# Last group of an MLP's second layer in three passes of 352 tokens, with the norm and the store following pass by pass

## The reference, cut to what matters

```python
h2 = rms_norm(x, lp['norm_pre_mlp'])
ff = jnp.square(jax.nn.relu(h2 @ lp['mlp_w1'])) @ lp['mlp_w2']
x = x + rms_norm(ff, lp['norm_post_mlp'])
```

## Time and profile before

| | |
|---|---|
| Median of 3 runs | 2189.09 us (2188.5 to 2189.5) |
| The profiled execution | 2189.16 us |
| Its span, first to last instruction | 2187.4 us |
| Mean granted TensorE clock | 0.97 |
| Busy: PE, DVE, ACT, POOL | 2034.9, 953.0, 516.4, 708.4 us |

### The profile page before, as it was taken

One profiled execution on the slowest core, in us unless ns is written; L12 is line 12 of the kernel. 1 busy time (PEld: TensorE's weight loads), 2 busy tenths in 40 slices (PEclk: granted clock), 3 DMA queues, 4 the chain that ended last, 5 costly groups with the idle time before them and its releaser, 6 DMA issues.

```text
span 2187.4 us, 32684 instructions
## 1 busy us (share of the span) xinstructions
PE 2034.9 (93%) x13822; PEld 1915.7 (88%) x13822; DVE 953.0 (44%) x1204; ACT 516.4 (24%) x687; POOL 708.4 (32%) x352
## 2 busy tenths in 40 slices
PE   4999999999999978888999996799999999999993
PEld 4999899999898956567999995799999999999992
DVE  7894431244455425553355813842313222231336
ACT  4212211333343335554200112320101001010100
POOL 0231111111111123332456644443434433344340
PEclk8999999999999989999999997899999999999996
DMA  3323337366676423302344321211111111111123
GB/s 131 98 93 108 103 101 229 129 215 201 203 235 205 139 90 90 91 26 79 117 166 144 129 101 39 98 39 49 49 40 49 39 49 40 49 48 40 49 69 119
DMA packets 144563, 223.48 MB, mean 102 GB/s; under 512 B 33808, under 2 KB 98576, under 8 KB 144432
## 3 DMA queue, kind: packets, MB, share of 16 engines
q1 hardware_dynamic: 132336, 193.42, 28.3%
q10 hardware_dynamic: 12096, 28.12, 3.5%
HBM read 173.84 MB, written 45.56 MB: 100 GB/s over the span
## 4 chain that ended last, share of the span: by engine, by line
PE 88%; DVE 7%; issue 2%; ACT 1%; DMA 1%; POOL 0%; SPq 0%; DVEq 0%; POOLq 0%
PE ps L1484 75%; PE ps L1677 3%; PE ps L1713 2%; PE ps L1701 1%; DVE sm L1302 1%; PE ps L1504 1%; PE ps L1623 1%; DVE resid L1405 1%; PE ps L1585 1%; PE ps L1604 1%; DVE n_rstd L989 1%; ACT pt L856 1%; DVE n_tmp L1403 1%; PE ps L1513 1%; DVE n_sum L981 1%
## 5 line engine op out<-in xcount | busy, mean ns | idle before, releaser
L638 POOL TENSOR_TENSOR w_hi<-w_raw,zeros 128x1024 fp32r<-128x1024 f32 x94 | 227.1, 2416 | 588.3 <-PE ps L1484 532.9
L1484 PE MATMUL ps<-op_hi,w_hi 128*128 128x352 f32 x1536 | 345.8, 334 | 9.2 <-DVE op_lo L1345 4.9
L629 POOL TENSOR_TENSOR w_lo<-w_raw,w_hi 128x1024 fp32r<-128x1024 f32 x54 | 135.5, 2509 | 651.6 <-ACT w_hi L714 651.6
L1484 PE MATMUL ps<-op_lo,w_hi 128*128 128x352 f32 x1536 | 334.6, 326 | 0.0
L1484 PE MATMUL ps<-op_hi,w_lo 128*128 128x352 f32 x1536 | 333.0, 325 | 0.0
L1484 PEld LDWEIGHTS ps<-op_hi,w_hi 128*128 128x128 f32 x1536 | 261.0, 190 | 20.6 <-issue 14.4
L1484 PEld LDWEIGHTS ps<-op_lo,w_hi 128*128 128x128 f32 x1536 | 263.8, 189 | 0.0
L1484 PEld LDWEIGHTS ps<-op_hi,w_lo 128*128 128x128 f32 x1536 | 262.8, 189 | 0.0
L640 POOL TENSOR_TENSOR w_lo<-w_raw,w_hi 128x1024 fp32r<-128x1024 f32 x94 | 251.9, 2680 | 7.4
L1484 PE MATMUL ps<-hid_hi,w_hi 128*128 128x352 f32 x1056 | 230.1, 326 | 9.3 <-issue 8.6
L1484 PE MATMUL ps<-hid_lo,w_hi 128*128 128x352 f32 x1056 | 230.0, 326 | 0.0
(11 more groups left out here) (244 smaller groups left out, 2336.1 us busy)
## 6 DMA issues: line engine op xcount, KB each, us to landing
w_raw<-in_w SPq DMA_DIRECT2D x148, 512.0 KB, 3.6
kc<-in_k_cache SPq DMA_DIRECT2D x48, 448.0 KB, 5.2
vc<-in_v_cache SPq DMA_DIRECT2D x48, 448.0 KB, 6.6
out_keep<-stage ACTq DMA_DIRECT2D x24, 528.0 KB, 2.7
tmp_gate_d<-stage ACTq DMA_DIRECT2D x24, 528.0 KB, 4.0
gate_t<-tmp_gate_d SPq DMA_DIRECT2D x24, 528.0 KB, 3.7
qkv<-out_keep SPq DMA_DIRECT2D x18, 512.0 KB, 4.9
acc<-in_x SPq DMA_DIRECT2D x8, 528.0 KB, 6.6
```

What stands on the lines that cost most here:

```text
L629: pool.tensor_tensor(w_lo[:, b].rearrange("p k m -> p (k m)"), w_raw[:, b], w_hi[:, b].rearrange("p k m -> p (k m)").bitcast(F32), ALU.sub ...
L638: pool.tensor_tensor(hi.rearrange("p (a m) -> p a m", a=2), w_raw[:, b].rearrange("p (a m) -> p a m", a=2), zeros[:].unsqueeze(1).broadcas ...
L1484: mm = pe.matmul(ps[:, 3 * dst + q, 0:BLK], w[:, b, w0 + n], x[:, k, q * BLK:(q + 1) * BLK], start=(n == 0 and part == 0), stop=(n == len( ...
```

## The change

The last group (line 1801) no longer goes tile by tile over all tokens, but in three passes q of 352 tokens, each over the eight output tiles n. Since every pass needs all the weights, the four halves of the last two pairs are split into buffers of their own (`lw_hi`, `lw_lo`) in area B, as soon as the last `up` is done (`UP_DONE`) instead of when a half of `w_hi` has been read. The residual goes to `res_y`, also in area B, and its eight loads are issued behind the last weight load. The tiles use six single banks in turn (bank 6 is for the total of the squares), and a tile waits until DVE has added the one six before. DVE waits for both of GpSimd's last splits and all eight loads before its first sum. The sum of squares, total, root, reciprocal and the eight rows of a pass are written out between the tiles of the next pass (`LATER` says after which tile which row), and SP stores 24 pieces of 128 x 352 instead of 8 slabs.

```diff
+CH_USES = USES[P_MLP + 6] - USES[P_MLP + 2]
+UP_DONE = USES[P_MLP + 2] + (NCH - 2) * CH_USES + 2
+P_LAST = len(PAIRS) - 2
+LAST_BANKS = 6
+LATER = [[], [], [], [0], [1], [2], [3], [4]]
...
+        lw_hi = at("B", 0, "lw_hi", [P, 4, KD, P], F32R)
+        lw_lo = at("B", 16384, "lw_lo", [P, 4, KD, P], F32R)
+        res_y = at("B", 32768, "res_y", [P, KD, N])
+        ff_sq = [stage[:, 0, n * BLK:(n + 1) * BLK] for n in range(2)]
+        ff_rs = stage[:, 0, 2 * BLK:]
+        ff_tmp = w_raw[:, 0, 0:BLK]
...
 # SP
-            sy.wait_ge(mm_ready[0], USES[-1] - KD // 2 + 1)
+            for b in range(2):
+                sy.wait_ge(mm_ready[b], UP_DONE)
             for k in range(KD):
-                if k == FCH:
-                    sy.wait_ge(mm_ready[1], USES[-1])
-                    sy.wait_ge(mm_ready[0], USES[-1])
-                sy.dma_start(resid[:, k], t["x2_d"][:, k]).then_inc(x2_in, 16)
-            for k in range(KD):
-                sy.wait_ge(y_done, k + 1)
-                sy.dma_start(t["y"][:, k], resid[:, k]).then_inc(y_out, 16)
-            sy.wait_ge(y_out, 16 * KD)
+                sy.dma_start(res_y[:, k], t["x2_d"][:, k]).then_inc(x2_in, 16)
+            for q in range(NBLK):
+                for k in range(KD):
+                    sy.wait_ge(y_done, KD * q + k + 1)
+                    sy.dma_start(t["y"][:, k, piece(q)], res_y[:, k, piece(q)]).then_inc(y_out, 16)
+            sy.wait_ge(y_out, 16 * KD * NBLK)
...
 # GpSimd
-            with pool.Fori(0, NCH - 1) as c:
-                for n in range(4):
-                    pair(c * 4 + first + n, PAIRS[first + n - 1], c * per + USES[first + n - 1])
-            run(len(PAIRS) - 1, len(PAIRS))
+            with pool.Fori(0, NCH - 2) as c:
+                pairs_of(c, range(4))
+            pairs_of(NCH - 2, range(3))
+            pool.wait_ge(mm_ready[0], UP_DONE)
+            for m in range(4):
+                split(P_LAST + m // 2, m % 2, (1, UP_DONE), (lw_hi[:, m], lw_lo[:, m]))
...
 # ACT
-            squares(n_ff, acc, lambda k: act.wait_ge(mm_free[k % 2], USES[-1] - KD // 2 + k // 2 + 1))
-            root(n_ff)
+            for q in range(NBLK):
+                for n in range(KD):
+                    last_square(q, n)
+                    if q and n == 1:
+                        last_root(q - 1)
+            last_root(NBLK - 1)
...
 # DVE
-            sums(last + per, n_ff)
-            inverse_root(n_ff)
+            def last_sum(q, n):
+                x = KD * q + n
+                dve.wait_ge(last_mm, x + 1)
+                v.tensor_tensor(acc[:, n, piece(q)], acc[:, n, piece(q)], ps[:, x % LAST_BANKS, 0:BLK], ALU.add).then_inc(last_kept, 1)
...
+            def last_inverse(q):
+                dve.wait_ge(n_ff.rs, q + 1)
+                v.reciprocal(stage[:, 1, piece(q)], ff_rs).then_inc(n_ff.h, 1)
+                dve.wait_ge(n_ff.h, q + 1)
+                dve.wait_ge(last_kept, KD * (q + 1))
+
+            def last_row(q, k):
+                wait(dve, y_done, KD * q + k)
+                v.scalar_tensor_tensor(out=ff_tmp, in0=acc[:, k, piece(q)], scalar=gains[:, 3, k:k + 1],
+                                       in1=stage[:, 1, piece(q)], op0=ALU.mult, op1=ALU.mult).then_inc(last_rows, 1)
+                dve.wait_ge(last_rows, KD * q + k + 1)
+                v.tensor_tensor(res_y[:, k, piece(q)], res_y[:, k, piece(q)], ff_tmp, ALU.add).then_inc(y_done, 1)
+
+            for b in range(2):
+                dve.wait_ge(w_split[b], len(PAIRS))
             dve.wait_ge(x2_in, 16 * KD)
-            add_normed(n_ff, 3, y_done)
+            for q in range(NBLK):
+                for n in range(KD):
+                    last_sum(q, n)
+                    if q >= 2 and n == 0:
+                        last_row(q - 2, 5)
+                    if n:
+                        last_square(q, n - 1)
+                    if q >= 2 and n in (1, 2):
+                        last_row(q - 2, 5 + n)
+                    if q and n == 2:
+                        last_inverse(q - 1)
+                    if q:
+                        for k in LATER[n]:
+                            last_row(q - 1, k)
+                if q == NBLK - 1:
+                    last_row(q - 1, 5)
+                last_square(q, KD - 1)
+            for k in range(6, KD):
+                last_row(NBLK - 2, k)
+            last_inverse(NBLK - 1)
+            for k in range(KD):
+                last_row(NBLK - 1, k)
...
 # TensorE
-            down(p1 + 4 * c + 4, 1, FCH * (c + 2), u1 + (c + 1) * per)
-            sum_squares(n_ff, USES[-1])
+            def last_tile(q, n):
+                m, x = n // 2, KD * q + n
+                te.wait_ge(w_split[m % 2], P_LAST + m // 2 + 1)
+                if x < LAST_BANKS:
+                    te.wait_ge(mm_free[x // 3], u1 + (c + 1) * per)
+                else:
+                    te.wait_ge(last_kept, x - LAST_BANKS + 1)
+                for k in range(FCH):
+                    for part, (w, y) in enumerate(((lw_hi, mid_hi), (lw_hi, mid_lo), (lw_lo, mid_hi))):
+                        mm = pe.matmul(ps[:, x % LAST_BANKS, 0:BLK], w[:, m, FCH * (n % 2) + k], y[:, FCH + k, piece(q)],
+                                       start=(k == 0 and part == 0), stop=(k == FCH - 1 and part == 2))
+                mm.then_inc(last_mm, 1)
+
+            def last_total(q):
+                te.wait_ge(n_ff.added, KD * (q + 1))
+                wait(te, n_ff.rs, q)
+                pe.matmul(ps[:, 6, 0:BLK], ones[:], pre_rstd[:, piece(q)], start=True, stop=True).then_inc(n_ff.sum, 1)
+
+            te.wait_ge(hid_l, FCH * NCH)
+            for q in range(NBLK):
+                for n in range(KD):
+                    last_tile(q, n)
+                    if q and n == 1:
+                        last_total(q - 1)
+            last_total(NBLK - 1)
```

More of the change, by code:

```diff
@@ L208, in hybrid_layer, with piece @@
         mid_lo = at("A", AREA // 2, "mid_lo", [P, 2 * FCH, N], F32R)
+        lw_hi = at("B", 0, "lw_hi", [P, 4, KD, P], F32R)
[4 more added lines that the diff above has]
+        ff_tmp = w_raw[:, 0, 0:BLK]
+        def piece(q):
+            return slice(q * BLK, (q + 1) * BLK)
         class NormTiles:
@@ L353, in hybrid_layer @@
         go = sem("go")
+        last_mm, last_kept, last_rows = sem("last_mm"), sem("last_kept"), sem("last_rows")
         hid_z, hid_f, hid_h, hid_l, hid_r = (sem("hid_" + x) for x in ("z", "f", "h", "l", "r"))
@@ L630, in low_of, with split @@
                                    w_hi[:, b].rearrange("p k m -> p (k m)").bitcast(F32), ALU.subtract).then_inc(w_split[b], 1)
-            def split(i, b, used):
-                if used:
-                    pool.wait_ge(mm_ready[used[0]], used[1])
+            def split(i, b, used, to=None):
+                pool.wait_ge(mm_ready[used[0]], used[1])
                 pool.wait_ge(w_loaded[b], 16 * (i + 1))
-                hi, lo = (w[:, b].rearrange("p k m -> p (k m)") for w in (w_hi, w_lo))
+                hi, lo = (w.rearrange("p k m -> p (k m)") for w in (to or (w_hi[:, b], w_lo[:, b])))
                 pool.tensor_tensor(hi.rearrange("p (a m) -> p a m", a=2), w_raw[:, b].rearrange("p (a m) -> p a m", a=2), zeros[:].unsqueeze(1).broadcast_to([P, 2, KD * P // 2]), ALU.add).then_inc(w_half, 1)
@@ L683, in _, with pairs_of @@
             first, per = P_MLP + 3, USES[P_MLP + 6] - USES[P_MLP + 2]
-            with pool.Fori(0, NCH - 1) as c:
-                for n in range(4):
-                    pair(c * 4 + first + n, PAIRS[first + n - 1], c * per + USES[first + n - 1])
-            run(len(PAIRS) - 1, len(PAIRS))
+            def pairs_of(c, ns):
+                for n in ns:
+                    pair(c * 4 + (first + n), PAIRS[first + n - 1], c * per + USES[first + n - 1])
+            with pool.Fori(0, NCH - 2) as c:
[4 more added lines that the diff above has]
+                split(P_LAST + m // 2, m % 2, (1, UP_DONE), (lw_hi[:, m], lw_lo[:, m]))
         @block.scalar
@@ L959, in _, with last_square, last_root @@
                 hidden(FCH * (NCH - 1) + n, n, 1, stage[:, 0])
-            squares(n_ff, acc, lambda k: act.wait_ge(mm_free[k % 2], USES[-1] - KD // 2 + k // 2 + 1))
-            root(n_ff)
+            def last_square(q, n):
+                x = KD * q + n
+                act.wait_ge(last_kept, x + 1)
+                wait(act, n_ff.added, x - 1)
+                s.activation(ff_sq[x % 2], acc[:, n, piece(q)], ACT.Square).then_inc(n_ff.sq, 1)
+            def last_root(q):
+                act.wait_ge(n_ff.sum, q + 1)
+                wait(act, n_ff.h, q)
+                s.activation(ff_rs, ps[:, 6, 0:BLK], ACT.Sqrt, bias=EPS, scale=1.0 / D).then_inc(n_ff.rs, 1)
+            for q in range(NBLK):
[4 more added lines that the diff above has]
+            last_root(NBLK - 1)
         @block.vector
@@ L1466, in _, with last_square @@
             sums(last + 2)
-            sums(last + per, n_ff)
-            inverse_root(n_ff)
```

(15 more changed lines are left out.)

## The result

The changed kernel takes 2172.59 us (median of 4 runs, 2171.15 to 2173.63) against 2189.3 (4 runs, 2188.5 to 2192.88): a ratio of 0.992, 95% interval 0.9903 to 0.9937. Forecast was 2173.5, range 2167 to 2180. The profiled execution took 2173.45 us for a span of 2171.7.

What follows compares the result with a forecast made beforehand. TensorE bounds the kernel up to its last matmul, then DVE: gapless from 2122.8 for 46.3 us to 2169.1, plus 2.6 for the last store gives span 2171.7; with 1.76 outside and the median adjustment, 2173.5 us, range 2167 to 2180.

Steps and rivals of the forecast that it cites:

- TensorE to the start of DVE's gapless stretch: Last group from 2100.8 until TensorE ends pass 1's third tile at 2122.8, at 1.947 us per tile.
- DVE's 80 instructions: From 2122.8 DVE runs 14 sums, 15 adds, 3 reciprocals and 24 rows without a gap: 46.3 us, ending at 2169.1.
- The last store: Final store at the kernel's end is 176 KB, not 528: 2.6 us instead of 3.1, with landing about 2.2.
- one bank: Last group: 12 successive matmuls adding into a single bank cost nothing extra; upper bound 2 us.
- the slack of 7 us: Residual loads land at about 2105; TensorE needs DVE's first sum only at 2112.5, so the wait costs nothing.
- One cover: Last pass's total, root and waits lie beside two leftover rows of pass 1 (2.3 us) on DVE, so cost nothing.
- my upper bound of 1.30: Last pass's 352-column ones-matmul for the total of squares takes 0.62 us, or 1.30 at half clock.
- No overlap: Rival: short DVE instructions never start before their predecessor ends, 45 joints give nothing back; +3.6 us, 2177.1; chance 0.17.
- DVE keeps pace: Rival: short DVE instructions are cheaper, only the last pass follows TensorE's end at 2148.7; time 2167.7; chance 0.06.
- x2 late: Rival: residual loads land at 2116 to 2125, TensorE stalls at tile 6 for 4 to 13 us; 2177 to 2186; chance 0.05.
- splits late: Rival: GpSimd's weight splits don't come forward, TensorE stalls 18 us at tile 6; about 2191.8; chance 0.03.
- Fixed cost: Rival: each DVE instruction costs 0.42 us fixed or more, not 0.158, making the chain 21 us longer, 2194.5; chance 0.04.

Runs made afterwards that it cites:

- x_pass2: Changed kernel plus eight unused 352-column DVE adds, one ahead of each sum of the last pass; last 1056-column sum to span end 73.5 us, against 70.05.
- late_split: Changed kernel with GpSimd's last split held until the sixth tile of the last group; last 1056-column sum to span end 77.9 us, against 70.05.
- sq_pool: sq_pe with GpSimd doing two of the last pass's eight rows, ACT multiplying their gain in; 2174.17 us, ratio 0.9928.
- no_adds: Changed kernel without the 21 DVE adds of squares (norm wrong, only time used); last 1056-column sum to span end 66.4 us, against 70.05.
- rows_end: Changed kernel with all 24 rows behind the last pass instead of between tiles; last 1056-column sum to span end 81.4 us, against 70.05.
- tiles_only: Kernel before with only the four splits and eight residual loads brought forward, no passes; 2189.75 us against 2190.08, ratio 0.9999.
- x_pass0: Changed kernel plus eight unused 352-column DVE adds, one ahead of each sum of pass 0; last 1056-column sum to span end 70.04 us, against 70.05.
- sq_pe: Changed kernel with squares summed by TensorE matmuls instead of DVE adds, rows fitted into the next pass; 2172.35 us, ratio 0.9916.
- two_banks: Changed kernel with two output tiles made together per pass, their matmuls alternating between two banks; last 1056-column sum to span end 73.2 us, against 70.05.
- blocks: Changed kernel with the other products also going block by block of 352 tokens into one bank, not three in turn; 2172.14 us.

## Why the prediction was right

**The sum, term by term.** By S I had forecast 2171.7 - 2100.82 = 70.9; it is 70.05. TensorE to the start of DVE's gapless stretch: 22.0 forecast, 21.7 measured (a tile takes 1.92, not 1.947; the inline total cost 0.59). DVE's 80 instructions: 46.3 forecast, 46.1 measured; the add 0.52, the scalar form 0.58, the reciprocal 2.35 are what the line through other sizes and the row of the very size said; one of the 15 adds is a copy of 0.34, which I had priced as an add. The last store: 2.6 forecast, 2.3 measured, because 176 KB land in 1.8, not 2.2. That the two spans both read 2171.7 is partly luck: this execution reached the last group 0.8 us later than the one of before.

**Removed, added, moved.** The matmuls cost nothing extra in one bank. The splits ended at 2088, 2093, 2098 and 2103 for 2087, 2092, 2097 and 2102. The residual was there at about 2107.6, not 2105: the loads issued at 2094.0 and took 13.6 us where I had taken 12; the slack of 7 us was 4 to 5, and the cost was nothing, as said. TensorE ended at 2149.1 for 2148.7. One cover was thinner than I thought: the root ended at 2157.58 and DVE started the last reciprocal at 2157.64, so 0.06 us more would have shown. The ones-matmul took 1.54, over my upper bound of 1.30. That this term cost nothing is in part luck.

**The rivals.** *No overlap*: the sum at 2128.52 lasts 0.51 and the next instruction starts at 2128.95, 0.08 ahead of its end, just as at 1056 columns. The Trainium skill's section "The DRAIN you can't avoid" goes on to say that an instruction that is not held starts earlier; I had left that out of the rival, and these rows agree with it, not with the sentence that I took. *DVE keeps pace*: no, a gapless 46 us; x_pass2 shows it from the other side. *x2 late* and *splits late*: neither came about, but late_split shows that I had them too cheap, since I priced a stall without the clock: 5.0 forecast for it, 7.9 measured. *Fixed cost*: an add of 352 columns takes 0.52, so it has the 0.158 of the others. The 2.40 us that I gave in its favour I put down to the GpSimd split beside it; sq_pool shows such a stretching at this size, the 1056-column case was not run apart.

**What the steps did not say.** That DVE's work counts only where it is the bound was used for pass 0, but not thought through for fewer instructions: no_adds gave 3.6 for some 6. Which part of the change brings what was not asked; rows_end and tiles_only answer it: 0 for the weights forward, 5.2 for the passes, 11.4 for the rows between the tiles.

## What to carry to other kernels

A tail that goes one engine at a time can be cut into passes and laid beside the matmuls, and its price is then read from the side engine: count its instructions from the point where it no longer waits, at their size, with 0.08 us back where one does not need its predecessor. Find that point before adding or removing work: ahead of it added work is free as long as it fits into the gaps (eight adds in x_pass0), and removing work can move the point itself (no_adds). When a change takes away slack (a bank, a tile of lag), look for old waits that this slack was covering.

## What was not expected of the hardware

- After 5.6 us without work, TensorE's granted clock was 0.50, and its matmuls kept 0.29 us from start to start for about 4.5 us of work; the stall of 5.6 cost 7.9 (late_split). In sq_pe, with 4.5 us of stalls spread over three waits, it fell too (0.60 and 0.55 in two stretches of 2 us).
- Beside a GpSimd instruction, with all operands in SBUF, DVE's instructions took 1.13 us instead of 0.58 and 0.52 (sq_pool).
- The last group's matmuls start 0.160 us apart in the changed kernel and in two_banks, 0.161 in blocks and 0.162 in tiles_only, and the other products 0.162 in either order; open.
